# Half of the last product's output tiles without the sampled tokens: GpSimd gathers their rows, VectorE adds them and makes w_lo

## What is computed

```python
s = einsum('chpe,hpne->chpn', q, sub_keys)      # 8 heads, 2 halves, 128 keys
ts, ti = top_k(s, 16)
cs, ci = top_k(all sums of two halves, 16)      # 16 experts of 16384, by head
idx = i1 * 128 + i2
gate = softmax(cs)
a = einsum('cd,chkd->chk', x, peer_u[idx])
act = gelu(a) * gate
out = einsum('chk,chkd->cd', act, peer_v[idx])  # then the last layer norm
```

## Time and profile before

| what | value |
|---|---|
| median of 3 runs | 2319.62 us (2319.2 to 2319.89) |
| profiled execution, first to last instruction | 2318.2 us |
| PE busy | 2301.9 us, 99% |
| VectorE, ScalarE, GpSimd busy | 61%, 38%, 73% |
| read from and written to HBM | 416.40 and 43.28 MB |

### The profile page before, as it was taken

How to read it: one execution, slowest core, us unless ns; L and a number is a source line. 1 busy time by engine, 2 the same in 40 slices (tenths; PEclk the granted TensorE clock), 3 DMA queues, 4 the chain that set the end, 5 groups by cost and what they waited for, 6 DMA issues and landing times.

```text
span 2318.2 us, 48204 instructions
## 1 busy us (share of the span) xinstructions
PE 2301.9 (99%) x17575; PEld 2293.4 (99%) x17575; DVE 1419.4 (61%) x2373; ACT 882.9 (38%) x1109; POOL 1702.8 (73%) x702
## 2 busy tenths in 40 slices
PE   9999999999999999999999999999999999999997
PEld 9999999999999999999999999999999999999997
DVE  3974564355569954656565640766666777666655
ACT  5444453345544443333333333333333333333334
POOL 4876677776677777677676767777777778777775
PEclk9999999999999999999999999999999999999998
DMA  7564446654455555666666668766666666666643
GB/s 255 168 200 146 145 143 206 213 173 154 146 164 194 185 191 184 217 215 211 211 209 213 208 216 257 282 205 206 209 215 220 217 213 206 208 206 217 199 164 114
DMA packets 141275, 458.25 MB, mean 198 GB/s; under 512 B 14448, under 2 KB 37232, under 8 KB 140656
## 3 DMA queue, kind: packets, MB, share of 16 engines
q1 hardware_dynamic: 116944, 416.42, 55.6%
q10 hardware_dynamic: 24264, 40.93, 4.8%
HBM read 416.40 MB, written 43.28 MB: 198 GB/s over the span
## 4 chain that ended last, share of the span: by engine, by line
PE 95%; DVE 4%; ACT 0%; issue 0%; ACTq 0%; DVEq 0%
PE ps L1412 30%; PE ps L1413 30%; PE ps L1418 30%; PE ps L1700 1%; DVE F L1010 1%; PE ps L1453 1%; DVE F L1011 1%; PE ps L1626 1%; PE ps L1645 0%; DVE b_lo L1024 0%; PE ps L1460 0%; DVE R L1039 0%; DVE R L1073 0%; PE ps L615 0%; ACT R L964 0%; PE ps L1551 0%
## 5 line engine op out<-in xcount | busy, mean ns | idle before, releaser
L707 POOL TENSOR_TENSOR w_lo<-raw,w_hi 128x1024 fp32r<-128x1024 f32 x692 | 1694.3, 2470 | 599.4 <-ACT w_hi L734 568.4
L734 ACT ACTIVATE w_hi<-raw 128x1024 fp32r<-128x1024 f32 x690 | 692.8, 1052 | 686.1 <-PE ps L1418 652.5
L1412 PE MATMUL ps<-a_hi,w_hi 128*128 128x288 f32 x3072 | 824.8, 295 | 0.0
L1413 PE MATMUL ps<-a_lo,w_hi 128*128 128x288 f32 x3072 | 822.6, 294 | 0.0
L1412 PE MATMUL ps<-b_hi,w_hi 128*128 128x288 f32 (+1 forms) x2432 | 655.1, 295 | 0.4 <-ACT w_hi L734 0.4
L1413 PE MATMUL ps<-b_lo,w_hi 128*128 128x288 f32 (+1 forms) x2432 | 653.0, 295 | 0.0
L1412 PEld LDWEIGHTS ps<-a_hi,w_hi 128*128 128x128 f32 x3072 | 577.7, 188 | 2.4 <-issue 2.2
L1413 PEld LDWEIGHTS ps<-a_lo,w_hi 128*128 128x128 f32 x3072 | 577.9, 188 | 0.1
L1418 PE MATMUL ps<-a_hi,w_lo 128*128 128x288 f32 x3072 | 467.2, 294 | 0.0
L1412 PEld LDWEIGHTS ps<-b_hi,w_hi 128*128 128x128 f32 x2432 | 457.1, 188 | 0.9 <-issue 0.8
L1413 PEld LDWEIGHTS ps<-b_lo,w_hi 128*128 128x128 f32 x2432 | 457.8, 188 | 0.1
(11 more groups left out here) (238 smaller groups left out, 1256.4 us busy)
## 6 DMA issues: line engine op xcount, KB each, us to landing
raw<-in_peer_u SPq DMA_DIRECT2D x256, 512.0 KB, 4.3
raw<-in_peer_v SPq DMA_DIRECT2D x256, 512.0 KB, 4.0
raw<-in_w_in SPq DMA_DIRECT2D x96, 512.0 KB, 3.9
gelu_scratch<-F ACTq DMA_DIRECT2D x32, 576.0 KB, 5.7
gate_scratch<-g_stage ACTq DMA_DIRECT2D x36, 512.0 KB, 6.0
F<-gelu_scratch SPq DMA_DIRECT2D x32, 576.0 KB, 5.7
raw<-in_w_out SPq DMA_DIRECT2D x32, 512.0 KB, 3.7
raw<-in_w_query SPq DMA_DIRECT2D x32, 512.0 KB, 3.7
```

The costliest lines, as they stand in the source:

```text
L707: pool.tensor_tensor(wl[:, j, s], raw[:, j, s], wh[:, j, s].bitcast(F32), ALU.subtract).then_inc(lo_ready, 1)
L734: act.activation(wh[:, k, s], raw[:, k, s], ACT.Copy).then_inc(hi_ready, 1)
L1412: pe.matmul(out, w, mh(k), start=(n == 0), stop=False)
L1413: pe.matmul(out, w, ml(k), start=False, stop=False)
```

## The change

**Fewer columns.** `v_cols` says how many token columns a unit's tiles have in the last product: 288 for the units 0 to 3 of a block, and 256, the prompt alone, for units 4 to 7. `product`, called by `v_pair` in place of `pairs`, and `take` use it.

**The sampled tokens of units 4 to 7.** 32 tokens by 128 picks are 4096 rows. They are put on 128 partitions (4 groups of 32 tokens, two heads each) by 32 slots (`SLOTS`). After the routing VectorE works out 32 addresses on each partition (E1, E2, 26 small instructions), and later the table VIDX of 8 row pieces by slot. GpSimd, once the first product is done, issues for each slot 8 indirect DMAs of 128 rows of 512 bytes and one of 128 gelu values, into a ring of 2 slots; 288 DMAs in all. VectorE waits for a slot's 9 DMAs, multiplies gelu by gate, and adds 1024 columns, scaled, to ACC (`add_slot`). In blocks 0 to 13 that stands at units 3 and 7, in block 14 at units 1, 3, 5 and 7. In block 15 eight fp32 matmuls of 32 columns (ACC by a 0/1 table) put the sums into the columns 256 to 287 of the finished banks; the additions into R have 288 columns there again. Slots 0 and 1 may be fetched at once, each later one when the slot two before is added.

**w_lo.** For units 0 to 119 of `peer_v` VectorE makes it (`lower`, semaphore `lo_dve`), after the gating and ahead of the two additions. GpSimd makes it for all units before and for units 120 to 127, after its last gather. SyncE's loads wait on `lo_dve` accordingly; the block pieces keep their places between the loads. ScalarE's instructions are unchanged.

The core of the diff:

```diff
+SPARSE = 4
+DENSE = 8 - SPARSE
+ROWS = 2 * SPARSE
+SLOTS = PH * TOPK // 4
+RING = 2
+V_LAST = 120
...
+                  ("ratio", PG * 16), ("iota", 128), ("token", 1), ("spread", NS)):
...
...
+        with nc.sbuf_tensor("sample_rows", [P, RING, ROWS * P], F32) as VROWS:
+            pass
...
+        E1, o_ab = carve(o_ab, SLOTS)
+        E2, o_ab = carve(o_ab, SLOTS)
+        EG, o_ab = carve(o_ab, SLOTS)
+        EU, EQ, EW = (GS[:, n, 0:SLOTS] for n in range(3))
+        ACC, o_ab = carve(head, ROWS * P)
+        VIDX, o_ab = carve(o_ab, SLOTS, ROWS)
+        AIDX, o_ab = carve(o_ab, SLOTS)
+        GELU, o_ab = carve(o_ab, SLOTS)
+        GATED, o_ab = carve(o_ab, RING)
+        VIDX, AIDX = VIDX.bitcast(U32), AIDX.bitcast(U32)
...
+        def v_cols(dj):
+            return T if dj < DENSE else SEQ
...
-            with sp.Fori(0, BLOCKS // 2 - 1) as i:
-                for s in range(2):
-                    for j in range(8):
-                        load(peer_v[16 * i + 8 * s + j], UNIT0["peer_v"] + 8 * s, 8 * i, j)
-                        if j < 4:
-                            block_piece(sp, 2 * i + s + 2, s, j, i)
-            stream(peer_v, UNIT0["peer_v"] + 112, 16, first=112)
+            def load_v(u, j, low, mark):
+                for h in range(2):
+                    sp.wait_ge(low, mark + h)
+                    sp.dma_start(raw[:, j % 2, h * HU:h * HU + HU], peer_v[u, :, h * HU:h * HU + HU])\
+                        .then_inc(loaded[2 * (j % 2) + h], 16)
+            def load_with_block(i, t):
+                u, s, j, i2 = 16 * i + t, t // 8 % 2, t % 8, i + t // 16
+                load_v(u, j, lo_dve, 2 * u - 3)
+                if j < 4 and not (isinstance(i, int) and u >= 112):
+                    block_piece(sp, 2 * i2 + s + 2, s, j, i2)
+            for j in range(2):
+                load_v(j, j, lo_ready, 2 * (UNIT0["peer_v"] + j) - 3)
+                block_piece(sp, 2, 0, j, 0)
+            with sp.Fori(0, BLOCKS // 2 - 2) as i:
+                for t in range(2, 18):
+                    load_with_block(i, t)
+            for t in range(2, 18):
+                load_with_block(BLOCKS // 2 - 2, t)
+            with sp.Fori(57, V_LAST // 2 + 1) as i:
+                for j in range(2):
+                    load_v(2 * i + j, j, lo_dve, 4 * i + 2 * j - 3)
+            for u in range(V_LAST + 2, 128):
+                load_v(u, u % 2, lo_ready, 2 * (UNIT0["peer_v"] + u - V_LAST - 2) + 1)
...
-            with pool.Fori(FIRST_UNITS // 2, UNITS // 2) as i:
+            with pool.Fori(FIRST_UNITS // 2, UNIT0["peer_v"] // 2) as i:
+                for j in range(2):
+                    lower(i, j)
+            v_rows = peer_v.rearrange("u p (r d) -> (u p r) d", d=P)
+            gelus = a_dram.rearrange("a p n -> (a p n)").unsqueeze(1)
+            pool.wait_ge(rows_named, 1)
+            pool.wait_ge(outs_done, OUT0["peer_v"] + 1)
+            for n in range(2):
+                pool.wait_ge(a_stored[n], 16 * BLOCKS + 1)
+            for k in range(SLOTS):
+                n = k % RING
+                if k >= RING:
+                    pool.wait_ge(slot_used, k - RING + 2)
+                for r in range(ROWS):
+                    pool.indirect_dma_start(VROWS[:, n, r * P:r * P + P], None, v_rows,
+                                            bass.IndirectOffsetOnAxis(ap=VIDX[:, k, r:r + 1], axis=0))\
+                        .then_inc(row_in[n][r], 16)
+                pool.indirect_dma_start(GELU[:, k:k + 1], None, gelus,
+                                        bass.IndirectOffsetOnAxis(ap=AIDX[:, k:k + 1], axis=0))\
+                    .then_inc(gelu_in[n], 16)
+            with pool.Fori((UNIT0["peer_v"] + V_LAST) // 2, UNITS // 2) as i:
                 for j in range(2):
                     lower(i, j)
             norm_pool(pool)
...
+            ve.wait_ge(r_idx, 1)
+            for g in range(4):
+                for src, dst in ((I1, E1), (I2, E2), (GA, EG)):
+                    mark = own.inc(ve.tensor_copy(dst[32 * g:32 * g + 32].rearrange("p (h k) -> p h k", h=2),
+                                                  src[TC - NS:TC, CH - 1, 2 * g:2 * g + 2, :]))
+            ve.wait_ge(dve, mark)
+            eu, eq, ew = (t.bitcast(U32) for t in (EU, EQ, EW))
+            def part(shift, mask, quotient):
+                ve.tensor_scalar(eq, eu, shift, None, ALU.logical_shift_right)
+                link(ve.tensor_scalar(ew, eu, mask, None, ALU.bitwise_and))
+                link(ve.tensor_copy(quotient, eq))
+                link(ve.tensor_copy(EQ, ew))
+            link(ve.tensor_copy(eu, E1))
+            part(3, 7, E1)
+            link(ve.scalar_tensor_tensor(out=E1, in0=E1, scalar=float(8 * P * KT), in1=EQ, op0=ALU.mult, op1=ALU.add))
+            link(ve.scalar_tensor_tensor(out=E1, in0=E2, scalar=float(KT), in1=E1, op0=ALU.mult, op1=ALU.add))
+            part(2, 3, EU)
+            link(ve.scalar_tensor_tensor(out=E2, in0=EU, scalar=float(P), in1=E2, op0=ALU.mult, op1=ALU.add))
+            link(ve.tensor_scalar(EQ, EQ, float(T), C("token"), ALU.mult, ALU.add))
+            link(ve.scalar_tensor_tensor(out=E2, in0=E2, scalar=float(4 * T), in1=EQ, op0=ALU.mult, op1=ALU.add))
...
             def take(o, j, i):
+                n = v_cols(j // 2)
                 ve.wait_ge(outs_done, OUT0["peer_v"] + i + o + 2)
-                ve.tensor_tensor(R[:, j, :], R[:, j, :], ps[:, ROT[(o + 2) % 4], 0:T], ALU.add).then_inc(ev_dve, 1)
+                ve.tensor_tensor(R[:, j, 0:n], R[:, j, 0:n], ps[:, ROT[(o + 2) % 4], 0:n], ALU.add).then_inc(ev_dve, 1)
+            def lower(u, j):
+                for h in range(2):
+                    ve.wait_ge(hi_ready, 2 * (UNIT0["peer_v"] + u) + h + 1)
+                    s = slice(h * HU, h * HU + HU)
+                    ve.tensor_tensor(wl[:, j, s], raw[:, j, s], wh[:, j, s].bitcast(F32), ALU.subtract)\
+                        .then_inc(lo_dve, 1)
+            def add_slot(i, n):
+                k, b = 4 * i + n, n % RING
+                for r in range(ROWS):
+                    ve.wait_ge(row_in[b][r], 16 * (2 * i + n // RING + 1))
+                ve.wait_ge(gelu_in[b], 16 * (2 * i + n // RING + 1))
+                link(ve.tensor_tensor(GATED[:, b:b + 1], GELU[:, bass.ds(k, 1)], EG[:, bass.ds(k, 1)], ALU.mult))
+                ve.wait_ge(slot_used, k + 1)
+                ve.scalar_tensor_tensor(out=ACC, in0=VROWS[:, b, :], scalar=GATED[:, b:b + 1], in1=ACC,
+                                        op0=ALU.mult, op1=ALU.add).then_inc(slot_used, 1)
             ve.wait_ge(g_ev, 8 * WITH + 1)
+            link(ve.memset(ACC, 0.0))
+            for r in range(ROWS):
+                ve.tensor_scalar(VIDX[:, :, r], E1, float((DENSE + r // 2) * P * KT + 8 * (r % 2)), None, ALU.add)
+            link(ve.tensor_copy(AIDX, E2))
+            ve.sem_inc(rows_named, 1)
             ve.wait_ge(blk_in[0], 64)
             for e in range(8):
                 gate(0, e)
             ve.wait_ge(y_init, 1)
-            def v_block(i, s):
+            lower(0, 0)
+            def v_block(i, s, slots):
                 ve.wait_ge(blk_in[1 - s], 64 * (i + s + 1))
@@ -1372,15 +1496,19 @@
                 for u in range(8):
                     if u < 7:
                         gate(1 - s, u + 1)
-                    for j in range(2):
-                        take(16 * s + 2 * u + j, 2 * u + j, 32 * i)
+                    if not isinstance(i, int) or 16 * i + 8 * s + u + 1 < V_LAST:
+                        lower(16 * i + 8 * s + u + 1, (u + 1) % 2)
+                    take(16 * s + 2 * u, 2 * u, 32 * i)
+                    if u in slots:
+                        add_slot(i, slots[u])
+                    take(16 * s + 2 * u + 1, 2 * u + 1, 32 * i)
             with ve.Fori(0, BLOCKS // 2 - 1) as i:
-                own.start(i, 32)
+                own.start(i, 36)
                 for s in range(2):
-                    v_block(i, s)
+                    v_block(i, s, {3: 2 * s, 7: 2 * s + 1})
                 own.stop(BLOCKS // 2 - 1)
-            v_block(BLOCKS // 2 - 1, 0)
+            v_block(BLOCKS // 2 - 1, 0, {1: 0, 3: 1, 5: 2, 7: 3})
...
+                lo_sem, lo_base = low or (lo_ready, 2 * u)
...
-                            pe.wait_ge(lo_ready, 2 * u + t // 8 + 1)
+                            pe.wait_ge(lo_sem, lo_base + t // 8 + 1)
                         last = pe.matmul(out, wl[:, slot, t * P:t * P + P], mh(k), start=False,
                                          stop=(n == len(tiles) - 1))
-                last.then_inc(outs_done, 1)
+                if ends:
+                    last.then_inc(outs_done, 1)
...
+            def v_pair(u, s, j, dj, low, final=False):
+                n = v_cols(dj)
+                for o in range(2):
+                    bank = ROT[(2 * j + o + 2) % 4]
+                    pe.wait_ge(ev_dve, DVE_EV0["peer_v"] + 2 * u + o - 3)
```

(24 more changed lines are left out.)

13 lines of the change are left out of this document (9 added, 4 removed).

## The result

The changed kernel took **2403.39 us** (2400.97 to 2404.93, 4 runs) beside 2319.76 for the kernel before: ratio 1.036 [1.035, 1.037], slower by 84 us, where 2275 was forecast. Its profiled execution took 2403.35 us, its span is 2401.5. So there are two results to explain, and both are in what follows.

What follows compares the result with a forecast made beforehand. TensorE, busy 99% of the span, was taken to bound the kernel. 2318.2 - 46.7 + 1.5 = 2273.0 us, 2274.4 against the median of the runs, plus 0.6 for a hitch: 2275 us, range 2270 to 2315.

Steps and rivals of the forecast that it cites:

- the one on the gathers: GpSimd's nine indirect DMAs a slot in the last product: hidden, cost 0; at 2.41 us each some 5 to 10 us.
- c: GpSimd's price of one indirect DMA: taken as about 1.2 us, between 0.33 and 2.41; it decides at 2.65 us.
- The gain: PE's last product: 3072 matmuls go from 288 to 256 columns, 15.2 ns less each, -46.7 us; columns alone -41.0.
- The fp32 matmuls for which I had added 1.5: PE's eight added fp32 matmuls of 32 columns: between nothing and 1.5 us, the upper bound taken.
- The 0.6 for a hitch at the first slot: Start of the last product: 0.6 us added to the sum for a hitch at the first slot of gathers.
- w_lo on VectorE: Last product: VectorE makes w_lo at 1.23 us a half and keeps up, 4 us to spare before PE; cost 0.
- The routing's small instructions: VectorE's 26 instructions before the one-hot copies: cost 0, up to some 15 us if each took 2 us.
- The DMA engines: Last product: 32768 pieces add 150 us on 16 engines; share 0.65 becomes 0.69, 0.9 at most; cost 0, thinnest margin.
- GpSimd held out by VectorE: Rival, `add_slot` waits in blocks 0 to 14: VectorE slows gathers to 3.2 us, +147, 2420 us; chance 0.16.
- The spacing that follows no columns: Rival, PE's last product: matmul spacing does not follow columns; no gain 2321 us, in the middle 2298; chance 0.04.
- the waits at both ends: Rival, first slots and block 14: waits at both ends only, c from 2.0 to 2.6, 2282 to 2295 us; chance 0.08.
- the late weights: Rival, last product: gathers crowd the loads, each of 15 blocks loses 1 to 3 us, 2290 to 2320; chance 0.12.

Runs made afterwards that it cites:

- e1: The changed kernel with GpSimd's 288 indirect DMAs left out and only their semaphores counted up: 2286.46 us, 0.9855 of the kernel before.
- e12: The changed kernel as it stands, measured a third time, on another chip: 2288.70 us, 0.9864 of the kernel before.
- e5: e1 with 31 unused columns behind the two new constants, so PE's moving operands start 256 bytes later than in the kernel before: 2278.83 us, 0.9825.
- sets 1 and 3: Two of six sets of follow-up runs, on chips A and C, each beside the kernel before; the changed kernel took 2430.59 us in set 3.
- e10: The changed kernel with gathers of slots 1 to 27 in rows of three and 31 unused columns behind the constants: 2298.21 us, 0.9908.
- e3: The changed kernel with each row gather of slots 1 to 27 waiting for one more output tile of TensorE: 2306.29 us, 0.9945.

## Why the prediction was wrong, point by point

**The step that failed** is the one on the gathers, which takes c as "about 1.2 us" and ends with "Cost 0 at my value". Its number was right: mostly 0.94 us and 0.30 to the next, 1.25 in all. But it asked only whether GpSimd keeps up with VectorE. That GpSimd's DMAs could stop TensorE, which waits for none of them, was in no term and in no rival; the issue of a DMA had been priced as time on its own queue alone. By the sum of distances this costs 114 us in the profiled execution (118 less the 4 of the kernel before), 117 by e1; without them the kernel takes 2289 (e12), inside the range of 2270 to 2315, 14 above the forecast.

**The gain.** 240 tiles took 756.3 us before. The forecast makes that 709.8 (47 us less, of which 239 of 240 parts lie between the first addition and the last); e5 shows 714.8, e12 721.7. So -46.7 was really -41.5 with the operands where they had been, which happens to be the lower bound, the columns alone: the tiles of 256 columns last 2.83 us there, 118 ns a matmul and not 116.6. The 117 ns of four one-hots in a row were a fair price for 256 columns, but not to the last ns for a stream with three kinds of matmul. By the estimate from the section on the back-to-back issue gap in the Trainium skill (TensorE: Matmul & The Clock Gate) it would have been 13 us; the trace disagrees, with 118.0 ns at 256 columns and 131.8 at 288 in e5.

**A term that was missing.** The table of constants grew by 33 columns. I read the change for what it adds to each engine and not for what it moves in memory. Price 7.6 us (e1 against e5; 8.5 in the two profiled executions: 5.0 in the last product, 3.3 ahead of its first addition, 0.2 behind).

**The sum of what differs in e12**: +11.9 us between the first and the last addition, +4.5 ahead of the first (1498.0 against 1493.5). The fp32 matmuls for which I had added 1.5 cannot be seen: from the last addition to the end of the span it is 68.1 us, and was 68.4. The 0.6 for a hitch at the first slot is no separate term either: the hitch is there (VectorE waits 6.0 us for slot 0, and PE once for w_lo behind it, 0.7 us), but it lies within the 11.9. 11.9 + 4.5 - 0.3 - 1.5 - 0.6 = 14.0, of the 13.7 to be explained. Of the 11.9, 5.0 are the gain that was taken too large (e5), 5.0 the moved operands (e1 against e5) and 1.9 the gathers with their hitch (e12 against e1).

**What held.** w_lo on VectorE costs nothing: 1.22 us a half, and PE waits for it 0.7 us in the whole of e12. The routing's small instructions cost nothing; PE's first one-hots even start at 898.8 in the first run, before 899.8. The DMA engines carry it: the share is 0.72 in e12 from 1700 to 1900 us (0.65 before, forecast 0.69), and the bytes cost 2.3 us. The 32768 pieces are 9216 packets on the page, with the gelu values, in 2.2% of the engines' span, 50 us on 16 engines in e12 where 150 had been added. VectorE waits once for a gather, at slot 0, 3.3 us in the first run and 6.0 in e12.

**The rivals.** "GpSimd held out by VectorE" gave 2420 us, close to what was measured on two chips, but for another reason. Its price c stayed at 1.25 where 2.65 was wanted. Single gathers do take up to 1.97 us in place of 0.94 beside VectorE, with little effect: in e12 the 42 over 1.4 us have VectorE's w_lo beside them for 80% of their time, those under 0.96 us for 7%. The Trainium skill (DMA: Bandwidth & Descriptors, SWDGE vs HWDGE vs iDMA) says that VectorE in its 2-port mode locks GpSimd out of the part of SBUF to which GpSimd writes its descriptors. That w_lo runs in this mode no run shows, so the trace agrees in direction only. The sign to look for, VectorE waiting for row DMAs at every slot, is absent. A rival that gives the right time is not confirmed by it. The spacing that follows no columns did not occur. Of the waits at both ends there is the 0.7 us at slot 0, and of the late weights little: ScalarE waits for raw 7.9 us in all in e12, 5.1 before, and PE not for it.

## What to carry to other kernels

Price a new kind of instruction on every engine that shares something with it, not only on its own: if the trace of before has no row for it, its side effects have no bound either, and the range must say so. When PE stands still in the middle of a tile with "issue" as the only releaser, look at what the other queues do in the 10 us before, and try spacing that work out before changing PE's code. Look also at how soon the engines that wait for PE are released: here that was late before any start of a matmul was. And a change to a table in SBUF moves what stands behind it: look at the offsets of PE's operands before and after, as 132 bytes cost 7.6 us here, and run a kernel that stops on a second chip before its loss or its cure is believed.

## What the runs showed of the hardware that was not expected

- Nine indirect DMAs of 128 rows in a row, mostly 1.25 us apart, stopped TensorE for 2.2 to 6.8 us a row on three of seven occasions of measuring (the first and sets 1 and 3); nine at 1.5 us did not. The first long distance between matmuls came 7.4 to 10.6 us after the start of a row of nine that stands alone, the longest in such a row was 0.7 to 1.8 us, and 2.8 us in a row of 27, which cost 20 us. Three in a row cost nothing in the same sets, 73 times in e10 and 24 in e3. Eight plain DMAs of as many bytes in 4.3 us cost nothing.
- In the first run PE's finished tiles were reported late, by up to 5.0 us, from 3.1 us after a row's start on, while its matmuls still started 0.12 us apart. The engines that wait for these tiles started as late.
- The same program had these stops on some chips and not on others, and one chip that had shown them with two kernels showed none an hour later with two others. The medians of the kernel before agree within 0.03% throughout.
- Moving operands that start 132 bytes further on lengthen the groups of one-hot matmuls from 6.79 to 6.84 us and the last product by 5.0 us in 715; 256 bytes on, the groups are as before.
- A gather of 128 pieces of 64 bytes is as long on GpSimd as one of 512 bytes (1115 ns on the mean); with 32 indices it is 0.87 us in place of 0.95 at the median.
